# Sampled rows' weight stream: two tiles at each visit of TensorE, through the same three slots

## The chip, the cores and the metric

The kernel runs on one core of one Trainium2 chip. The metric is the device time of one execution in microseconds, compared by the medians of several runs. Profiles are taken on the same program.

## What is computed

One layer step for two kinds of rows, with shared weights: 1024 prompt rows and 8 sampled rows (one new token for each of 8 sequences with 4096 cached positions). The reference, cut down:

```python
q, k, v, logf, u = project(x, w_in, b_f)        # 1024 -> 3*512 + 8 + 512
attn = fox_prompt(q, k, v, logf)                # or fox_sample over the paged cache
pool = pool_mix(u_ext, start_pos, w_pool, pool_scale)
mix = concat(attn, pool) @ w_o                  # 1024 x 1024
x1 = layer_norm(ALPHA * x + mix, ln1_g, ln1_b)
hid = silu(x1 @ w_gate) * (x1 @ w_up)           # 1024 -> 2816
ffn = hid @ w_down                              # 2816 -> 1024
return layer_norm(ALPHA * x1 + ffn, ln2_g, ln2_b)
```

All data are float32. The prompt rows' products are made of three fp32r products each (high and low parts of both operands); the sampled rows' products use plain float32.

## The kernel before, in words

**The order of the work.** After attention the kernel runs one long sequence that is counted in *units* u. A unit is six fp32r matmuls of 512 columns for the feed-forward of the prompt rows. The 22 tiles of the hidden width give segments G (gate, 8 units each), U (up, 8 units) and D (down, 16 units for a pair of tiles); `segments()` writes their order out. Each engine walks through the same u in a loop of its own (`for u in range(LAST)`, on TensorE `for seg in SEGS`), and what else is to be done stands at a chosen u in front of or behind the unit's own work. Nothing is scheduled at run time: an engine that has to wait at one u holds up all that stands behind it in its own queue.

**The sampled rows.** Their 8 rows are multiplied with `w_o`, `w_gate`, `w_up` and `w_down` inside this sequence, from u = 386 on. The weights come as a stream of 37 tiles of 1 MB (`STREAM`, L169): four tiles W of `w_o`, then for each group g of four hidden tiles four GU tiles (two for the last, g = 5), and D tiles of `w_down` for the group before. `SUNIT` (L171) and `sample_steps()` (L147) say at which u each tile is used; before the change W tiles stand at u = 386, 388, 390, 392, and the 33 others from u = 406 to 504, about three units apart.

- `sample_tile(step)` (L1483) on TensorE waits until the tile has landed and runs four float32 products of 512 columns (eight of 256 for the last two GU tiles). They stand in four groups of 32 columns of the array and write to PSUM bank 6 (W and D, L1511) or bank 7 (GU, L1498). The profile shows each product as two matmuls, so a tile is 8 matmuls of 512 columns (or 16 of 256). One place of u where tiles are used is called a *visit* here; the last matmul of each tile increments `t_used`.
- Two units after the last GU tile of a group (`SUMS`), `sample_sum(g)` (L1516) on TensorE adds the partial products up. In front of it ScalarE has to copy them out of PSUM (`sample_partials`, L1094 with its copy at L1101, at SUMS - 1); ScalarE does at the same u what is due there before: `tile_hi` (L1013, its cast at L1026) makes the high part of the prompt rows' next weights, and waits for TensorE to end the segment whose weights it replaces. At SUMS + 1 ScalarE and VectorE make the hidden values, on which the next group's first GU tile and the group's own D tiles wait.
- SyncE issues the loads. `stream_tile(n)` (L643, its DMA at L652) has `TS = 3` slots; from the fourth tile on it waits until tile n - 3 has been used, and stands at one unit after that tile's visit. `weight_tile(e)` (L592, L596) loads the prompt rows' weights, 0.5 MB each, and waits until GpSimd has made the low part (`rest`, L807) of the tile three before; at an equal u it stands in front of the stream's load.

**Around the visits.** At u = 395 to 404 VectorE makes the first layer norm of the sampled rows (L2018 to L2036), TensorE turns them at u = 404 (L1533), and the second norm follows u = 506. The two norms stay at their u in the change.

Of the kernel before, what the change touches and what calls it, by code (L numbers as in the profile page):

```python
# [146 lines left out]
def sample_steps():  # L147


    order = []  # L150
    for g in range(TGROUPS):
        order += [("GU", g, r) for r in range(parts("GU", g))]
        order += [("D", g - 1, r) for r in range(parts("D", g - 1))] if g >= 1 else []
    order += [("D", TGROUPS - 1, r) for r in range(parts("D", TGROUPS - 1))]
    units = {step: TSTART + SPAN_S * n // (len(order) - 1) + 3 * (n >= parts("GU", 0)) for n, step in enumerate(order)}
    return units, [units["GU", g, parts("GU", g) - 1] + 2 for g in range(TGROUPS)]


def parts(kind, g):
    full = 4 * g + 4 <= FT  # L160
    return {"GU": (2, 4), "D": (1, 2)}[kind][full]
# [3 lines left out]
MIX, RESID, SQRT1, SCALE1, FACTORS1, OFFSETS1 = (CSPAD + n for n in (2, 11, 12, 13, 14, 18))  # L165
TURN1, TURNED1, TSTART = (CSPAD + n for n in (20, 21, 22))
SPAN_S = BEGIN["D", NPAIR - 1] - 11 - TSTART
STEPS_S, SUMS = sample_steps()
STREAM = [("W", n, 0) for n in range(4)] + list(STEPS_S)  # L169
TINDEX = {step: n for n, step in enumerate(STREAM)}  # L170
SUNIT = {("W", n, 0): MIX + 2 * n for n in range(4)} | STEPS_S  # L171
NORM2 = BEGIN["D", NPAIR - 1] + 2
SAMPLE2 = max(SUNIT.values()) + 2
LNVEC2 = BEGIN["U", FT - 1] + 2
# [36 lines left out]
def build(nc, t):  # L211
    ctx = ExitStack()
    with ctx:
# [259 lines left out]
        def _(sp):  # L473
# [169 lines left out]
            def stream_tile(n):  # L643
                if n < 2:
                    sp.wait_ge(k_red, NB * NKP)
                    if n == 1:
                        sp.wait_ge(m_sub, 2 * NB)
                elif n < TS:
                    sp.wait_ge(v_used, NB * NCH - 1)
                else:  # L650
                    sp.wait_ge(t_used, n - TS + 1)
                sp.dma_start(TR[n % TS], t["ws"][n]).then_inc(t_ld[n % TS], 16)  # L652

            for u in range(LAST):
# [18 lines left out]
                for n in range(TS, len(STREAM)):  # L673
                    if SUNIT[STREAM[n - TS]] + 1 == u:
                        stream_tile(n)
# [470 lines left out]
        def _(pe):  # L1146
# [369 lines left out]
            def sample_sum(g):  # L1516

                pe.wait_ge(e_gs, g + 1)
                for i in range(min(4, FT - 4 * g)):
                    ins = pe.matmul(PSM[:, 7, 2 * NB * i:2 * NB * (i + 1)], gu_s[:, i * P:(i + 1) * P], gumask[:],  # L1520
                                    start=True, stop=True)
                ins.then_inc(e_sum, 1)

            def sample(u):
                if u in SUMS:
                    sample_sum(SUMS.index(u))
                for step, at in SUNIT.items():
                    if at == u:
# [667 lines left out]
```

## Time and profile before

| what | value |
|---|---|
| time, three runs | 1450.91 us median (1446.38 to 1454.49) |
| the profiled execution's own time | 1451.53 us |
| its span, first to last instruction | 1449.0 us |
| granted TensorE clock, mean | 0.979 of full speed |
| TensorE matmuls busy | 1374.7 us (95% of the span) |
| VectorE, GpSimd, ScalarE busy | 48%, 37%, 25% |
| moved by DMA | 255.81 MB, 177 GB/s |

The profiled execution lies 0.62 us above the median of the runs; 2.5 us of its time lie outside the span. Rows of TensorE are named PE (matmuls) and PEld (weight loads). A matmul's shown duration overlaps the next one's, since its end is modelled; distances between starts are what tells its cost. Several neighbours of one kind stand in one row of the timeline as x2, x4 and so on.

### The profile page before, as it was taken

The numbers are of one execution on the slowest core, as the hardware profiler recorded it, in microseconds if no ns is written. First come the engines' busy times: TensorE is split into PE (matmuls) and PEld (weight loads), VectorE is DVE, ScalarE is ACT, GpSimd is POOL, SyncE is SP. The second block draws the span as 40 slices with busy tenths as digits, with TensorE's granted clock in tenths as the row PEclk, the third lists the DMA queues.
The fourth block names the chain that finished last, engine by engine and source line by source line (L and its number), as shares of the span: only waits on it lengthen the run. The fifth ranks groups of instructions, "written<-read, shape, count | busy, mean of one in ns | idle before, by whom it ended". The sixth has DMA issues, their size and how long they took to land.

```text
span 1449.0 us, 21271 instructions
## 1 busy us (share of the span) xinstructions
PE 1374.7 (95%) x7605; PEld 1081.9 (75%) x7605; DVE 695.4 (48%) x1043; ACT 359.9 (25%) x527; POOL 533.7 (37%) x250
## 2 busy tenths in 40 slices
PE   7899979989989899999999999999999999999996
PEld 5888879989869886676767676776767666666665
DVE  4746765874355683353536262544523142221336
ACT  4524334343331223111021211121120111111016
POOL 1016464742210035545565556555530212111114
PEclk9999999999989999999999999999999999999998
DMA  7244482731036115867676867768574644566522
GB/s 261 91 150 136 136 253 83 234 115 51 1 108 230 59 67 170 271 198 259 208 253 198 265 209 226 257 203 267 192 237 145 201 140 142 191 225 217 209 88 117
DMA packets 111913, 255.81 MB, mean 177 GB/s; under 512 B 12864, under 2 KB 23233, under 8 KB 106424
## 3 DMA queue, kind: packets, MB, share of 16 engines
q1 hardware_dynamic: 102528, 247.79, 51.4%
q10 hardware_dynamic: 8320, 4.19, 1.0%
q0 software_dynamic: 960, 2.47, 0.5%
q8 instruction: 60, 0.98, 0.3%
q14 instruction: 45, 0.37, 0.1%
HBM read 244.38 MB, written 10.25 MB: 176 GB/s over the span
## 4 chain that ended last, share of the span: by engine, by line
PE 77%; DVE 6%; SPq 5%; DMA 4%; issue 4%; POOL 3%; ACT 2%; ACTq 0%; DVEq 0%; POOLq 0%
PE PSM L1414 28%; PE PSM L1432 16%; PE PSM L1172 8%; PE PSM L1362 6%; PE PSM L1454 4%; PE PSM L1238 3%; PE PSM L1185 3%; SPq L477 2%; SPq L482 2%; PE PSM L1224 2%; PE PSM L1498 2%; POOL WR L755 1%; DMA AR<-cache_v 1%; PE PSM L1393 1%; PE PSM L1511 1%
## 5 line engine op out<-in xcount | busy, mean ns | idle before, releaser
L807 POOL TENSOR_TENSOR WL<-WR,WH 128x1024 fp32r<-128x1024 f32 x55 | 131.5, 2392 | 545.2 <-ACT WH L1026 545.2
L1414 PE MATMUL PSM<-XH,WH 128*128 128x512 f32 x672 | 221.2, 410 | 0.0
L755 POOL TENSOR_TENSOR AR<-AR,QB 128x1024 f32<-128x1024 f32 x80 | 196.2, 2471 | 43.9 <-DMA AR<-cache_k 32.0
L1414 PE MATMUL PSM<-XL,WH 128*128 128x512 f32 x672 | 212.0, 397 | 0.0
L1414 PE MATMUL PSM<-XH,WL 128*128 128x512 f32 x672 | 211.9, 397 | 0.0
L1414 PEld LDWEIGHTS PSM<-XH,WH 128*128 128x128 f32 x672 | 120.1, 189 | 88.0 <-issue 65.7
L1957 DVE TENSOR_TENSOR ACC<-ACC,PSM 128x512 f32<-128x512 f32 x160 | 108.3, 683 | 153.3 <-PE PSM L1432 152.9
L1414 PEld LDWEIGHTS PSM<-XH,WL 128*128 128x128 f32 x672 | 127.1, 189 | 30.4
L1432 PE MATMUL PSM<-R 128*128 128x512 f32 x528 | 149.7, 392 | 0.0
L1414 PEld LDWEIGHTS PSM<-XL,WH 128*128 128x128 f32 x672 | 127.2, 189 | 30.0
L1432 PE MATMUL PSM<-WH,R 128*128 128x512 f32 x352 | 143.2, 407 | 3.8 <-DVE R L1948 3.8
L1026 ACT CAST WH<-WR 128x1024 fp32r<-128x1024 f32 x55 | 57.5, 1047 | 327.8 <-PE PSM L1414 238.9
L1172 PE MATMUL PSM<-XH,WH 128*128 128x344 f32 x384 | 135.7, 353 | 0.0
L1944 DVE TENSOR_TENSOR AR<-AR,PSM 128x1024 f32<-128x1024 f32 x22 | 26.9, 1221 | 208.6 <-PE PSM L1414 201.6
L1172 PE MATMUL PSM<-XH,WL 128*128 128x344 f32 x384 | 125.0, 326 | 0.0
L1172 PE MATMUL PSM<-XL,WH 128*128 128x344 f32 x384 | 124.9, 325 | 0.0
L1432 PEld LDWEIGHTS PSM<-R 128*128 128x128 f32 x528 | 99.6, 189 | 22.1
L1594 DVE TENSOR_REDUCE AR<-AR 128x16 f32<-128x1024 f32 x64 | 77.6, 1212 | 64.6 <-POOL AR L755 64.1
L964 ACT ACTIVATE AR<-AR,negm 128x128 f32<-128x128 f32 (+3 forms) x64 | 49.8, 777 | 184.4 <-DVE negm L1685 184.4
L1432 PEld LDWEIGHTS PSM<-WH,R 128*128 128x128 f32 x352 | 66.5, 189 | 36.3 <-DVE ACC L1957 11.3
L755 POOL TENSOR_TENSOR ACC<-ACC,QB 128x1024 f32<-128x1024 f32 x24 | 58.8, 2459 | 72.0 <-issue 25.2
L1454 PE MATMUL PSM<-AR,PR 128*8 128x512 f32 x512 | 74.0, 598 | 5.3 <-DMA AR<-cache_v 5.3
(257 smaller groups left out, 2231.1 us busy)
## 6 DMA issues: line engine op xcount, KB each, us to landing
AR<-cache_v SPq DMA_DIRECT2D x256, 256.0 KB, 3.5
AR<-cache_k SPq DMA_DIRECT2D x160, 256.0 KB, 3.4
AR<-ws SPq DMA_DIRECT2D x37, 1024.0 KB, 4.9
WR<-ffn SPq DMA_DIRECT2D x66, 512.0 KB, 5.3
ACC<-cache_k SPq DMA_DIRECT2D x48, 256.0 KB, 3.0
WR<-cache_k SPq DMA_DIRECT2D x48, 256.0 KB, 3.0
WR<-w_in SPq DMA_DIRECT2D x20, 512.0 KB, 4.6
WR<-w_o SPq DMA_DIRECT2D x5, 1024.0 KB, 5.0
```

Of the source, the lines that this page charges most:

```text
L755: pool.tensor_tensor(keys, keys, QB[:].rearrange("p (o n) -> p o n", o=1).to_broadcast([P, KP, AW]), ALU.mult).then_inc(k_mul, 1)
L807: pool.tensor_tensor(lo, WR[:, raw_weight(e), :], hi.bitcast(F32), ALU.subtract).then_inc(ffn_lo, 1)
L964: act.activation(L[x % 2][:, 0:w], L[x % 2][:, 0:w], ACT.Exp, scale=-1.0, bias=negm[:, x % 2:x % 2 + 1], accum_out=rsum[:, x % 2:x % 2 + 1 ...
L1026: act.copy(weight_slot(kind, f)[0], WR[:, raw_weight(e), :]).then_inc(ffn_hi, 1)
L1172: ins = pe.matmul(third(n, m), w[a][:, tile_slot(n), k * P:(k + 1) * P], x[b][:, k, m * TH:(m + 1) * TH], start=(k == 0 and (a, b) == PART ...
L1185: ins = pe.transpose(TB[:, i * P:(i + 1) * P], src(i), ident[:])
L1362: ins = pe.matmul(output_bank(n), (XH, XL)[a][:, k, i * P:(i + 1) * P], wo[b][k // 4][:, k % 4, :], start=(r == 0 and at == 0), stop=(r == ...
L1414: ins = pe.matmul(out[:, hc], (hi, lo)[a][:, k * P:(k + 1) * P], x[b][:, k, hc], start=(k == 0 and n == 0), stop=(k == KC - 1 and n == 2))
L1432: ins = pe.matmul(PSM[:, 2 + n % 4, :], R2[:, 2 * r + a, i * P:(i + 1) * P], w[b][:, half * HALF:(half + 1) * HALF], start=(r == 0 and m = ...
L1454: ins = pe.matmul(PSM[32 * j:32 * j + H, 6, :], PR[:, c * CH + j, :], VR[c % 2][:, j * AW:(j + 1) * AW], start=(c == 0), stop=last, skip_g ...
L1594: dve.tensor_reduce(out[:, c * KP:(c + 1) * KP, :].rearrange("p j h -> p (j h)"), keys.rearrange("p (a n) -> p a n", n=HD), AX.X, ALU.add) ...
L1957: dve.tensor_tensor(cols, cols, PSM[:, 2 + n % 4, :], ALU.add).then_inc(d_free, 1)
```

## The change

Both formulas that place the tiles are changed, so that tiles 2m and 2m + 1 of the stream stand at one u, in front of the same unit. The four W tiles now stand at 386, 386, 390, 390. The 33 others stand in 16 pairs and a single tile, the pairs five or six units apart, from 406, 411, 420, 426, 432, 438 to 498, and the last tile at 504 as before. That gives 19 visits for 37 tiles. What is derived from it follows: the loads of two tiles stand together behind each visit; the sums' places (`SUMS`) become 413, 428, 446, 464, 482, 494 where they were 416, 431, 449, 467, 485, 497. The number of slots, the tiles, the matmuls and all waits are the same.

```diff
@@ sample_steps()
-    units = {step: TSTART + SPAN_S * n // (len(order) - 1) + 3 * (n >= parts("GU", 0)) for n, step in enumerate(order)}
+    units = {step: TSTART + SPAN_S * (n // 2) // (len(order) // 2) + 3 * (n >= parts("GU", 0)) for n, step in enumerate(order)}
     return units, [units["GU", g, parts("GU", g) - 1] + 2 for g in range(TGROUPS)]
@@
-SUNIT = {("W", n, 0): MIX + 2 * n for n in range(4)} | STEPS_S
+SUNIT = {("W", n, 0): MIX + 4 * (n // 2) for n in range(4)} | STEPS_S
```

## Rows read from the trace of the kernel before

**Rows 1.** Page: the chain that ended last, shares of the span by line

```profile
PE PSM L1414 28%; PE PSM L1432 16%; PE PSM L1172 8%; PE PSM L1362 6%; PE PSM L1454 4%; PE PSM L1238 3%; PE PSM L1185 3%; SPq L477 2%; SPq L482 2%; PE PSM L1224 2%; PE PSM L1498 2%; POOL WR L755 1%; DMA AR<-cache_v 1%; PE PSM L1393 1%; PE PSM L1511 1%
```

**Rows 2.** Busy times by stretch: us, busy us of each engine, granted clock, DMA share, GB/s

```profile
1216.00:1410.00 194.00, 191.72 (x960) 127.27 (x960) 43.51 (x58) 26.59 (x35) 29.55 (x12) 1.00 0.55 193
```

**Rows 3.** Chain that ended last, in order of time: start, us, what

```profile
1315.37 4.40 PE PSM L1414 x18
...
1343.10 4.31 PE PSM L1432 x18
```

**Rows 4.** Timeline of PE, units of U and G: start, us, what

```profile
1191.82 0.63 PE L1414 MATMUL PSM<-XH,WH 128*128 128x512 f32 x2
...
1205.75 0.63 PE L1414 MATMUL PSM<-XH,WH 128*128 128x512 f32 x2
...
1241.49 1.06 PE L1498 MATMUL PSM<-AR,GB 128*32 128x512 f32 x8
...
1246.88 1.06 PE L1498 MATMUL PSM<-AR,GB 128*32 128x512 f32 x8
```

**Rows 5.** Timeline of PE in parts: the two packs of a 512-column tile

```profile
1231.06 0.64 PE L1498 MATMUL PSM<-AR,GB 128*32 128x512 f32 x4
...
1231.51 0.61 PE L1498 MATMUL PSM<-AR,GB 128*32 128x512 f32 x4
```

**Rows 6.** Timeline of PE in parts: third and fourth pack of a 256-column tile

```profile
1375.33 0.40 PE L1498 MATMUL PSM<-AR,GB 128*32 128x256 f32 x4
...
1375.54 0.40 PE L1498 MATMUL PSM<-AR,GB 128*32 128x256 f32 x4
```

**Rows 7.** Timeline of PE, the sums of groups 2 and 5

```profile
1293.85 0.62 PE L1414 MATMUL PSM<-XH,WL 128*128 128x512 f32 x2
1295.71 1.06 PE L1520 MATMUL PSM<-gumask_sb,QB 128*128 128x16 f32 x8 [1.24 <-ACT QB L1101]
...
1383.68 0.61 PE L1414 MATMUL PSM<-XH,WL 128*128 128x512 f32 x2
1385.34 0.62 PE L1520 MATMUL PSM<-gumask_sb,QB 128*128 128x16 f32 x4 [1.05 <-ACT QB L1101]
```

**Rows 8.** Timeline of ACT at the same two places

```profile
1294.14 1.03 ACT L1026 CAST R<-WR 128x1024 fp32r<-128x1024 f32 x1
1295.08 0.57 ACT L1101 COPY QB<-PSM 128x512 f32<-128x512 f32 x1
...
1384.92 0.36 ACT L1101 COPY QB<-PSM 128x256 f32<-128x256 f32 x1
```

**Rows 9.** The loads into the stream's slots, from issue to landing, all 37

```profile
DMA to landing us min/median/max: 4.7/4.9/7.3
```

**Rows 10.** Loads by line: KB, us to landing; issued at 1282.03, then at 1299.41

```profile
WR<-ffn SPq DMA_DIRECT2D x1, 512.0 KB, 5.7
...
AR<-ws SPq DMA_DIRECT2D x1, 1024.0 KB, 6.8
```

**Rows 11.** Timeline of SP behind the visit at u = 450

```profile
1296.69 2.67 SPq L596 DMA_DIRECT2D WR<-ffn  x2
1299.41 0.43 SPq L652 DMA_DIRECT2D AR<-ws  x1
```

**Rows 12.** Timelines of DVE and PE around the turn at u = 404

```profile
1196.44 1.21 DVE L2033 TENSOR_TENSOR AR<-AR 8x1024 f32<-8x1024 f32 x1
1201.86 1.22 DVE L1944 TENSOR_TENSOR AR<-AR,PSM 128x1024 f32<-128x1024 f32 x1 [4.21 <-PE PSM L1414]
...
1209.83 1.01 PE L1533 MATMUL PSM<-ident_sb,AR 8*128 8x8 f32 x8 [2.52 <-DVE AR L2036]
```

**Rows 13.** Busy times by stretch, behind that turn

```profile
1209.90:1216.10 6.20, 6.20 (x20) 4.65 (x20) 0.23 (x1) 0.00 (x0) 0.00 (x0) 0.50 0.22 82
```

**Rows 14.** Weight loads of the GU tiles: ns min/median/max, first and last start

```profile
L1498 PEld LDWEIGHTS PSM<-AR,GB x192: 106/109/154, 1216.2 to 1380.7; 128*32 128x32 f32 x192
```

## The prediction

> **What bounds the kernel now.** I read the page's chain first, then the busy times by stretch, the chain in order of time, and last the starts of single matmuls on PE, because only distances between starts tell what a visit costs.
>
> The chain that ended last runs mostly over PE [rows 1]. In the stretch that holds most of the stream, 1216 to 1410, PE is busy 191.7 of 194 us at the full granted clock, all others at most 23%, and the DMA engines 55% [rows 2]. There the chain is PE alone, the tiles' matmuls in turns with three units (18 matmuls) in 4.40 us for G and U or 4.31 us for D [rows 3]. So each us that PE is spared ends the kernel earlier, as long as no load and no other engine takes its place. The change adds and removes no matmul; what it can change is the cost of going into and out of the tiles, the places where PE waits, and whether tiles are there in time.
>
> **What a visit costs.** Ten units of G and U without a visit take 1205.75 - 1191.82 = 13.93 us, so a unit is 1.39 us [rows 4]. From one visit to the next with three units between them there are 1246.88 - 1241.49 = 5.39 us; less 3 x 1.39 a visit costs 1.21 us [rows 4]. I take 1.20, since a D stretch has slightly shorter units. 37 visits are 44 us.
>
> **What the second tile of a visit costs.** The matmuls of a tile go in packs of four that start together. The second pack of a 512-column tile starts 1231.51 - 1231.06 = 0.45 us behind the first [rows 5]. Two packs at that distance are 0.90 us, so 0.30 us of the visit are entry and exit. No visit of before has four packs of 512 columns, but the last GU tiles have four of 256: the last two are 1375.54 - 1375.33 = 0.21 us apart [rows 6]. For twice the columns that is 0.43 us (0.42 to 0.43 by rounding), 0.86 for the two packs. The second tile therefore adds 0.86 (by rows 6) to 0.90 us (by rows 5), and a merged visit saves 0.34 to 0.30 us. I take 0.34, since rows 6 show packs in the third and fourth place, with other weights than the two before them, which is exactly what a second tile is. The far ends: it may save nothing (the second tile also needs the landing of its load and pays its own entry), or, if half of the entry and exit were hidden as well, no more than 0.4. There are 18 merged visits: **18 x 0.34 = 6.1 us** (5.4 by rows 5; ends 0 and 7.2).
>
> The Trainium skill says (TensorEngine Tiling (Array Packing), Tiling Modes) that changing the tiling mode drains the array, while changing tiles within a mode does not. That gives the reason for an entry and an exit that one visit pays once, and no other number.
>
> **The sums.** Six times TensorE runs `sample_sum`, two units behind the last GU tile. At group 2 (u = 449) it starts at 1295.71, while the pair of matmuls before it started at 1293.85 and would let it start 0.46 us later: 1.4 us lost, released by ScalarE's copy. At group 5 (u = 497) the same gives 1385.34 - 1384.14 = 1.2 us [rows 7]. ScalarE was late there because the copy stands at u = 448 and 496, where two casts for new weights are due before it, and these wait for the end of a segment: the copy began at 1295.08 and 1384.92 right behind them [rows 8]. Groups 0, 1, 3 and 4 lose nothing. In the change the copies stand at u = 412, 427, 445, 463, 481, 493, the sums one unit later. The casts stay at 408, 416, 424, 440, 448, 456, 464, 472, 488, 496. None shares a u with a copy or stands directly in front of one; the nearest in front is three units (4.2 us) away, against at most two casts (2 us) and a silu. So both waits go: **2.6 us**. Ends: 0, if a new place waits (it would be behind another cast), and 2.6. What is late next at these places is nothing that PE needs soon: the low half of the hidden tile, needed a segment later.
>
> **Loads.** Tile 2m + 3 goes into the slot of tile 2m, and its load is released when that first tile of the visit is used, not at the visit's end: 1.1 us behind the visit's start, the 1.06 us of its matmuls [rows 4] and some hundredths for the signal. It is used as second tile of the next visit. From visit to visit lie 6 x 1.39 + 2.06 = 10.4 us (2.06 = 1.20 + 0.86), plus 0.89 until the second tile begins, less 1.1: 10.2 us are left. With five units (406 to 411) it is 8.8, and for W (four D units of 1.37) 7.3. The loads took 4.7 to 7.3 us, median 4.9 [rows 9]. Tile 2m + 4 is issued 0.9 us behind and has a whole period more. Two such loads stand behind each other now. A 0.5 MB load that was issued 1.2 us behind a stream tile landed after 5.7 us [rows 10], so a second load queues behind the first, by an amount that the longer time covers. I cost the loads at 0; what hides them is 2.9 us of slack even at the longest load seen, and for W 2.4 us at the median. Weight loads of the prompt rows that queue behind 2 MB are some 3 us later; the next user is 12 units or more away.
>
> One place is tight: at u = 451 SP first waits for GpSimd and issues two weight loads, at 1296.69 and 2.3 us later, and only then the stream's tile at 1299.41 [rows 11], which landed 6.8 us later [rows 10]. Unit 448 ended at 1294.31, where the sum could have started, and so began at 1292.92; the landing at 1306.2 is 13.3 us behind that. In the change the second tile at u = 456 begins 2 x 1.39 + 0.1 + 10.4 + 0.9 = 14.2 us behind it. 0.9 us of slack: at 0, end 1 us lost.
>
> **The turn at u = 404.** PE waits 2.52 us there for VectorE, and that wait [rows 12] stays: the norm's chain was through with L2033 at 1197.65 and VectorE then idle 4.21 us until PE ended U16. In the change the last W tile ends two units earlier but the chain still starts behind the last D unit: about 0.8 us later against PE, covered by these 4.2 us. Behind the wait the granted clock was 0.50, the 1.2 GHz level, for 6.2 us [rows 13]; that stretch can be a few us longer or shorter from run to run, and I put nothing on it. The tail (one tile at 504, norm at 506) is not moved.
>
> **Sum.** 6.1 + 2.6 = 8.7 us against the profiled execution's 1451.53: 1442.8 us. The median of the runs stands 0.6 lower, at 1450.91; I say 1442.2, 0.60% less. A measurement of this kernel can tell about 0.5% (7.3 us) from no change, so the forecast stands only 1.4 us beyond that line, and the three runs of before spread over 8.1 us.
>
> **Rivals.**
> 1. *The second tile's weight loads are not hidden.* Each pack loads 32 columns four at a time, 109 ns each [rows 14]. If two packs paid that in each merged visit, 0.22 of the 0.34 us would go: 18 x 0.12 + 2.6 = 4.8 us, 1446.1. Against it: third and fourth pack of rows 6 are 0.21 us apart although their weights are loaded meanwhile. Chance 0.08.
>  The Trainium skill has such a rule (TensorE: Matmul & The Clock Gate, Part 3, What overlaps and what doesn't): weight loads overlap running matmuls only if their row group differs, and all these tiles use all rows. By that rule this rival holds; the distances of rows 6 don't bear it out.
> 2. *The visit pays entry and exit per tile*, because the second tile's wait for its load breaks the stream: only the sums gain, 1448.3. Against it: each D unit also has waits that were long fulfilled, and its three units take 4.31 us without a gap [rows 3]. Chance 0.06.
> 3. *The sums wait at a new place*, or their gain is lost to another wait: 6.1 us alone, 1444.8. Chance 0.06.
> 4. *Slower: the tile in the second half of a visit lands late.* This is one mechanism: a load that shares the DMA engines with another 1 MB beside it. It decides from 10.2 us after issue on. If it landed after 12 us, 17 visits would lose 1.8 us each, 31 us, for 1442.2 + 31 = 1473; to be over 0.5% slower it takes 16 us in all, a landing after 11.1 us. Against it: longest load 7.3 us [rows 9], DMA engines 55% busy [rows 2], and more bytes in the same time are not moved. Chance 0.04.
>
> **Numbers.** Forecast 0.76. With the runs' spread it falls beyond 0.5% in about 7 of 10: 0.54, plus a little of rival 3, gives faster 0.56. Same: the rest of the forecast and rivals 1 to 3, 0.40. Slower 0.04. The range: down to 1438.0, which is 1450.9 less the far ends 7.2 + 2.6 and 3 us of the runs' spread; up to 1448.5, which takes in rivals 1 to 3.
>
> **What would show it.** Right: 19 groups x16 (two x32) of L1498 and L1511 but the last, about 2.06 us from entry to exit; packs 0.43 us apart; no wait of L1520 for ACT; landings below 10 us; the wait of 2.5 us in front of L1533 unchanged. Wrong: PE idle with DMA as the releaser in front of L1498 or L1511, a low granted clock between 1216 and 1410, or packs of a second tile 0.5 us and more behind the first's.

## The result, and the profile after

| | before | changed |
|---|---|---|
| median of 8 runs each | 1446.82 us (1442.58 to 1454.49) | 1436.22 us (1433.34 to 1441.16) |
| ratio, 95% interval | | 0.9922 (0.9895 to 0.9949) |
| two more comparisons (12 and 11 runs of the changed kernel) | | 0.9950 (0.9924 to 0.9976), 0.9938 (0.9914 to 0.9962) |
| profiled execution, span | 1451.53, 1449.0 us | 1433.34, 1431.5 us |

The change makes the kernel faster: all three intervals lie below 1. One more run of the last comparison, a slow one of 5730.55 us, is left out. The three comparisons have a mean ratio of 0.9937, that is 9.1 us of 1447; the forecast was 8.7 us, 0.60%. The forecast time and the range were nevertheless missed: 1436.22 lies below 1438.0. Why is told below; the larger part of it was not one of the terms of the sum.

The page of the changed kernel, its chain by line (it answers to [rows 1]):

```profile
span 1431.5 us, 21271 instructions
...
PE PSM L1414 30%; PE PSM L1432 16%; PE PSM L1172 8%; PE PSM L1362 6%; PE PSM L1454 4%; PE PSM L1238 3%; PE PSM L1185 3%; PE PSM L1224 2%; SPq L477 1%; PE PSM L1498 1%; SPq L482 1%; PE PSM L1393 1%; POOL WR L755 1%; PE PSM L1511 1%; DMA AR<-cache_v 1%
```

The share of the chain that goes over the stream's tiles fell (L1498 from 2% to 1%), and no other share moved by more than two points.

**The visits.** The chain in order of time shows two visits of the changed kernel, and the timeline of PE, cut into parts, the packs inside another one (start, us, what; only the starts are read, since the x at the end counts what the part held):

```profile
1295.49 1.85 PE PSM L1498 x16
1297.34 8.57 PE PSM L1414 x36
1305.91 1.85 PE PSM L1498 x16
```

```profile
1231.42 0.64 PE L1498 MATMUL PSM<-AR,GB 128*32 128x512 f32 x4
...
1232.30 1.03 PE L1498 MATMUL PSM<-AR,GB 128*32 128x512 f32 x6
...
1232.73 0.61 PE L1498 MATMUL PSM<-AR,GB 128*32 128x512 f32 x4
1233.27 0.73 PE L1414 MATMUL PSM<-XH,WH 128*128 128x512 f32 x2
```

The second tile begins 1232.30 - 1231.42 = 0.88 us behind the first, and its second pack 0.43 us later. From visit to visit with six units between lie 1305.91 - 1295.49 = 10.42 us; less 6 x 1.39 a double visit costs 2.08 us by these rounded rows (2.06 with the unit at 1.393). That is the forecast price.

**The sums.** In the list of who waited for whom, from the tiles' start on, TensorE's own waits for another engine are now only these (us in total, times, longest), and L1520 is not among them:

```profile
PE PSM L1432 <- DVE R L1948: 3.8, 1, 3.8
PEld PSM L1533 <- DVE AR L2036: 2.9, 1, 2.9
PE PSM L1533 <- DVE AR L2036: 2.5, 1, 2.5
```

Both waits of [rows 7] are gone, and the wait at the turn is the 2.5 us of [rows 12].

**The loads.** Issue to landing of all 37 loads into the slots:

```profile
DMA to landing us min/median/max: 4.7/6.4/8.4
```

Then the two that stand behind the weight loads at u = 451: the timeline of SP, the landing of each (KB, us), and the second tile's weight loads at u = 456 (timeline of PEld):

```profile
1289.64 0.91 SPq L652 DMA_DIRECT2D AR<-ws  x2
...
AR<-ws SPq DMA_DIRECT2D x1, 1024.0 KB, 5.7
...
AR<-ws SPq DMA_DIRECT2D x1, 1024.0 KB, 7.8
...
1296.30 0.13 PEld L1498 LDWEIGHTS PSM<-AR,GB 128*32 128x32 f32 x4 [0.30 <-issue]
```

The median rose from 4.9 to 6.4 us [rows 9], since the second load of a pair queues behind the first: behind the visit at u = 406 they landed 4.9 and 7.7 us after their issue. None is waited for. The first of the two loads at u = 451 is the second tile of u = 456; it landed at 1289.64 + 5.7 = 1295.3, 1.0 us before its use at 1296.30, where the forecast left 0.9. The other is the first tile of u = 462 and has a period more.

**The granted clock.** The busy times by stretch, columns as in [rows 2], behind the turn at u = 404:

```profile
1203.40:1209.60 6.20, 6.20 (x40) 3.80 (x41) 0.22 (x1) 0.00 (x0) 0.00 (x0) 1.00 0.40 103
```

Where the kernel before ran at 0.50 [rows 13], this execution ran at the full clock, behind the same wait. This, and an earlier start of the stream (1171.69 against 1177.49, with no changed instruction ahead of it), is what the two profiles' spans differ by beyond the forecast.

### The profile page after: what moved, and what is told of

It is laid out like the page before. It is cut to its first block, busy times and chain, and to the rows that moved or that the text cites. A ratio compares the mean times of both kernels' runs of the same rounds, so it can differ in the third digit from the quotient of the medians.

```text
span 1431.5 us, 21271 instructions
## 1 busy us (share of the span) xinstructions
PE 1359.9 (95%) x7605; PEld 1077.4 (75%) x7605; DVE 696.9 (49%) x1043; ACT 360.2 (25%) x527; POOL 534.1 (37%) x250
## 4 chain that ended last, share of the span: by engine, by line
PE 78%; DVE 8%; DMA 4%; SPq 3%; issue 3%; POOL 2%; ACT 2%; ACTq 0%; DVEq 0%; POOLq 0%
PE PSM L1414 30%; PE PSM L1432 16%; PE PSM L1172 8%; PE PSM L1362 6%; PE PSM L1454 4%; PE PSM L1238 3%; PE PSM L1185 3%; PE PSM L1224 2%; SPq L477 1%; PE PSM L1498 1%; SPq L482 1%; PE PSM L1393 1%; POOL WR L755 1%; PE PSM L1511 1%; DMA AR<-cache_v 1%
## 5 line engine op out<-in xcount | busy, mean ns | idle before, releaser
L1432 PE MATMUL PSM<-R 128*128 128x512 f32 x528 | 149.7, 392 | 0.0
L1432 PE MATMUL PSM<-WH,R 128*128 128x512 f32 x352 | 142.9, 406 | 4.8 <-DVE R L1948 3.8
L1432 PEld LDWEIGHTS PSM<-R 128*128 128x128 f32 x528 | 99.7, 189 | 22.4
L1944 DVE TENSOR_TENSOR AR<-AR,PSM 128x1024 f32<-128x1024 f32 x22 | 26.9, 1221 | 164.0 <-PE PSM L1414 157.0
L1432 PEld LDWEIGHTS PSM<-WH,R 128*128 128x128 f32 x352 | 66.5, 189 | 34.0 <-issue 17.8
```

The costliest lines, as they stand in the source:

```text
L1432: ins = pe.matmul(PSM[:, 2 + n % 4, :], R2[:, 2 * r + a, i * P:(i + 1) * P], w[b][:, half * HALF:(half + 1) * HALF], start=(r == 0 and m = ...
```

## Experiments

All profiles are compared over one stretch: from the start of the first tile to the start of the last row of L1432 on PE. It is 1437.12 - 1177.49 = 259.63 us for the kernel before and 1419.71 - 1171.69 = 248.02 us for the changed one:

```profile
1171.69 0.64 PE L1511 MATMUL PSM<-AR,GB 128*32 128x512 f32 x4
...
1419.71 0.84 PE L1432 MATMUL PSM<-R 128*128 128x512 f32 x3
```

"Low" below is the time in this stretch at the 1.2 GHz level, without the one behind the last wait, the 3.8 us of L1432 for VectorE. That one is 3.4 us long in every profile but e5's, where it is 6.8.

**e1: the pairs, with the sums where they were.**

```diff
-    return units, [units["GU", g, parts("GU", g) - 1] + 2 for g in range(TGROUPS)]
+    before = {step: TSTART + SPAN_S * n // (len(order) - 1) + 3 * (n >= parts("GU", 0)) for n, step in enumerate(order)}
+    return units, [before["GU", g, parts("GU", g) - 1] + 2 for g in range(TGROUPS)]
```

> The pairs of the change, but the sums, their copies and their silus at the units of before (416, 431, 449, 467, 485, 497). If the two parts of the sum are independent (visits 6.1 us, sums 2.6 us), this kernel keeps the visits' part alone: 19 visits of which 18 cost 2.06 us, the waits of L1520 for ScalarE's copy at groups 2 and 5 are back with 1.4 and 1.2 us, and the time is 2.6 us above the changed kernel's and some 6 us (0.4%) below the kernel before. Rival: the sums' waits came from the tile's late end and not from the casts in front of the copy; then they stay away here too, since the last GU tile now ends three units earlier, and the time equals the changed kernel's.

Measured: ratio 0.9958 (0.9928 to 0.9989), 1442.87 us, median of 12 runs. The waits for the copy are back at groups 2 and 5, 2.3 us on PE (and 3.1 us on PEld, in the same time) as in the kernel before, though the tile now ended three units earlier:

```profile
1295.03 1.06 PE L1521 MATMUL PSM<-gumask_sb,QB 128*128 128x16 f32 x8 [1.24 <-ACT QB L1102]
```

So they come from ScalarE's casts in front of the copy and not from the tile; the rival falls. And one thing that the prediction had not priced: the clock fell behind this wait, and the next visit, of 16 matmuls, took 2.94 us in place of 1.92 (busy times by stretch, then timeline of PE):

```profile
1211.40:1218.20 6.80, 6.79 (x24) 4.93 (x28) 0.22 (x1) 0.00 (x0) 0.00 (x0) 0.50 0.22 79
1296.80:1300.20 3.40, 3.40 (x16) 1.14 (x18) 2.70 (x2) 0.00 (x0) 1.52 (x1) 0.50 0.67 213
```

```profile
1298.09 2.94 PE L1512 MATMUL PSM<-AR,SC 128*32 128x512 f32 x16
```

**e2: the kernel before, with ScalarE's copy in front of the casts.** Only the order within one u is changed:

```diff
             for u in range(LAST):
                 b, o = divmod(u, WIN)
+                for g in range(TGROUPS):
+                    if SUMS[g] - 1 == u:
+                        sample_partials(g)
                 if u > 0 and u in TURN_U:
                     rows_hi(TURN_U[u])
...
                 for g in range(TGROUPS):
-                    if SUMS[g] - 1 == u:
-                        sample_partials(g)
                     if SUMS[g] + 1 == u:
                         sample_silu(g)
```

> The kernel before, with the single tiles, but at each unit ScalarE makes the copy for the sum before the casts that are due at the same unit. If the casts in front of the copy were what TensorE waited for, the waits of L1520 at groups 2 and 5 go (1.4 and 1.2 us) and the kernel is 2.6 us (0.2%) faster than before, with 37 visits of 1.20 us unchanged. Rival: the casts are only moved behind the copy and hold up something that TensorE needs soon (high part of the weights, hidden tile); then a new wait of about 0.5 us each stands elsewhere and the gain is nearer 1.5 us.

Measured: ratio 0.9998 (0.9970 to 1.0026). By time alone this tells nothing, since the expected 0.9982 and no change are both inside. By the profile the waits are gone; the sum of group 2 follows the last matmul pair at once, and the casts behind the copy hold up nothing: TensorE's list of waits has only those of the turn and of the last D segment (timeline of PE, then of ACT):

```profile
1288.94 0.63 PE L1415 MATMUL PSM<-XH,WL 128*128 128x512 f32 x2
1289.40 0.96 PE L1521 MATMUL PSM<-gumask_sb,QB 128*128 128x16 f32 x8
```

```profile
1286.66 0.59 ACT L1101 COPY QB<-PSM 128x512 f32<-128x512 f32 x1 [12.02 <-PE PSM L1499]
1288.27 1.06 ACT L1026 CAST WH<-WR 128x1024 fp32r<-128x1024 f32 x1 [1.02 <-PE PSM L1415]
```

**e3, e8, e10: the changed kernel again; e6, e7: the kernel before again.** No edit.

> The changed kernel once more, for a second profile. The profiled execution of the changed kernel had no stretch of low granted clock behind the turn at u = 404, the one of the kernel before had 6.8 us of it. If that is chance (where the wait falls in time), this profile may show 0, 3.4 or 6.8 us of it, and over the runs the change is worth about 8.7 us. Rival: the change removes it always, then every profile of the changed kernel is free of it and the change is worth about 11.5 us. Visits 2.06 us, no wait of L1520 for the copy in either case.

> A second profile of the kernel before, for the granted clock behind the turn at u = 404. If a low stretch there is chance, it may have 0, 3.4 or 6.8 us; if the kernel before always has it, 3.4 us or more again. From the first tile of the stream to the last product of TensorE: 257.2 us plus about 0.43 of each us at the low clock.

> A third profile of the kernel before, with the same expectations as for the second.

> A third profile of the changed kernel. Two profiles had no low clock behind the turn. If that is chance, this one may show 3.4 or 6.8 us; if the change removes it, none. The stretch from the first tile of the stream to the last product of TensorE: 248.5 us, and about 0.43 of each us at the low clock more.

> The changed kernel again, on one chip with e9, for the size of the change. If the parts found in the profiles are all of it (visits 6.1, sums 2.6 us, and a low clock behind the sum of group 2 in some executions of the kernel before, about 1 us in the mean), it is 9 to 10 us below the kernel before, a ratio of 0.993 to 0.994. Rival: the first measurement's 0.9922 was the true size; then 11 us and more.

Measured: e3 0.9950 (0.9924 to 0.9976), e10 0.9938 (0.9914 to 0.9962); e6, e7 and e8 are one execution each. Together with the others:

| profile | stretch, us | low behind the turn | low behind the sum of group 2 | stretch less 0.44 x low |
|---|---|---|---|---|
| before | 259.63 | 6.8 | 0 | 256.6 |
| e6, before | 258.35 | 0 | 3.4 | 256.9 |
| e7, before | 259.88 | 3.4 | 3.4 | 256.9 |
| changed | 248.02 | 0 | 0 | 248.0 |
| e3, changed | 248.04 | 0 | 0 | 248.0 |
| e10, changed | 248.03 | 0 | 0 | 248.0 |
| e8, changed | 251.04 | 6.8 | 0 | 248.0 |
| e1, pairs alone | 255.36 | 6.8 | 3.4 | 250.9 |
| e2, sums alone | 255.37 | 3.4 | 0 | 253.9 |

The price of a low us comes from e8 against the changed kernel: (251.04 - 248.02) / 6.8 = 0.44. The row of e8 behind its turn, and that of e7 behind its sum:

```profile
1206.20:1213.00 6.80, 6.80 (x24) 4.85 (x28) 0.23 (x1) 0.00 (x0) 0.00 (x0) 0.50 0.20 75
```

```profile
1293.90:1297.30 3.40, 3.40 (x13) 1.15 (x11) 3.01 (x2) 0.00 (x0) 1.83 (x1) 0.50 0.64 187
```

With that taken out, the three profiles of before agree within 0.3 us. The three of the changed kernel without a low stretch agree within 0.02 us; e8 gave the price and so checks nothing. The difference is 256.8 - 248.0 = 8.8 us, where the forecast has 8.7; e1 gives 5.9 us for the visits (forecast 6.1), e2 2.9 us for the sums (forecast 2.6), each from one profile. The low clock behind the turn comes and goes from one execution to the next in both kernels (2 of 3 profiles of before, 1 of 4 of the changed one), so it is not removed by the change; whether it comes less often is not shown by so few. Behind the sum of group 2 it fell in three of four profiles with that wait (before, e6, e7, e1), and in none of the others. Three quarters of 3.4 x 0.44 us is 1.1 us: a rough estimate, from four profiles, of what the change gains besides. 8.8 + 1.1 = 9.9 us are 0.9932, inside all three intervals. The rival of e10, 11 us and more, is not borne out, though its interval alone does not shut it out.

**e4: VectorE's last addition of the first sampled norm three units earlier.**

```diff
-MIX, RESID, SQRT1, SCALE1, FACTORS1, OFFSETS1 = (CSPAD + n for n in (2, 11, 12, 13, 14, 18))
+MIX, RESID, SQRT1, SCALE1, FACTORS1, OFFSETS1 = (CSPAD + n for n in (2, 11, 12, 13, 14, 15))
```

> The changed kernel with VectorE's last addition of the first sampled norm (L2036) at u = 399 in place of 404, in front of the prompt rows' product at u = 400. VectorE was idle for 3.4 us there. If the wait of 2.5 us in front of L1533 comes from that addition standing behind the hidden tile's low half in VectorE's queue, it goes: about 2.9 us less than the changed kernel, and also no low granted clock behind the turn in any profile. Rival: the addition waits for ln1_b to land and holds up the product at u = 400, so that half or more of the gain is lost.

Measured: ratio 0.9897 (0.9852 to 0.9941), 1431.12 us; stretch 245.43, 2.6 us less than the changed kernel's. By the constants (384 + 18, then 384 + 15) the addition moved from u = 402 to 399; the 404 of the expectation is the unit of the turn. It waited 2.0 us for `ln1_b`, as the rival has it, but in time that was idle, and held up nothing. The addition now fills VectorE's idle time and L1944 follows it (timeline of DVE):

```profile
1193.80 1.21 DVE L2036 TENSOR_TENSOR AR<-AR 8x1024 f32<-8x1024 f32 x1 [2.02 <-DMA AR<-ln_b]
1195.19 1.22 DVE L1944 TENSOR_TENSOR AR<-AR,PSM 128x1024 f32<-128x1024 f32 x1 [0.18 <-PE PSM L1414]
```

It took 1.21 us here, 3.38 where it stood before (why was not tried). No wait stands in front of L1533, and no low clock behind it.

**e5: the changed kernel with two slots for the stream.**

```diff
-TS = 3
+TS = 2
...
                 if u == (NB - 1) * WIN + VLOAD[-1]:
-                    stream_tile(2)
                     sp.wait_ge(v_used, NB * NCH)
```

> The changed kernel with two slots for the stream in place of three: both tiles of a visit are loaded behind the visit before. The first is issued 1.1 us and the second 2.0 us behind that visit's start; in the changed kernel such pairs landed 4.8 to 6.5 and 6.4 to 8.4 us after issue. Needed are they after 10.4 and 11.3 us (five units: 9.0 and 9.9; W: 7.5 and 8.4). So if loads have the slack that the prediction says, waits for loads come to at most 3 us in all, nearly all of them at W, at u = 411 and at u = 456, and the time is 0 to 3 us above the changed kernel's. Rival (a late second tile makes it slow): more than 1 us of wait at each of 17 visits, and 15 us or more above the changed kernel's.

Measured: ratio 0.9958 (0.9929 to 0.9987), 1442.38 us; stretch 250.83, 2.8 us above the changed kernel's. Waits for loads came up, few and short (who waited for loads of the stream; us, times, longest):

```profile
PEld PSM L1497 <- DMA AR<-ws: 3.7, 3, 2.5
PE PSM L1497 <- DMA AR<-ws: 1.6, 1, 1.6
PEld PSM L1510 <- DMA AR<-ws: 0.7, 1, 0.7
```

The four waits stand where the expectation puts them: at the second W visit, at u = 411 and at both tiles of u = 456. Only the last place costs PE anything. There the visit begins 0.2 us late and its second tile 2.66 us behind the first, in place of 0.88 (timeline of PE):

```profile
1304.70 1.07 PE L1497 MATMUL PSM<-AR,GB 128*32 128x512 f32 x8
...
1307.36 1.06 PE L1497 MATMUL PSM<-AR,GB 128*32 128x512 f32 x8 [1.59 <-DMA AR<-ws]
```

That is 2.0 of the 2.8 us; the other 0.8 is the longer low clock behind the last wait, which this profile alone has. So with a slot less the stream costs 2 us at one place, not the 15 of the rival. With three slots that place has 1.0 us left and all others more.

**e9: e4, and the last addition of the second sampled norm one unit earlier.**

```diff
-                if u == SAMPLE2 + 6:
+                if u == SAMPLE2 + 5:
                     dve.wait_ge(e_g1, 2)
```

> The kernel with VectorE's addition at u = 399 (as in e4) and also the last addition of the second sampled norm one unit earlier, at u = 511, in front of the prompt rows' last product at u = 512 instead of behind it. There it stood for 1.2 us in the chain to the last D segment. If VectorE's place in the queue is what counts, the wait in front of the last D segment falls from 3.8 to 2.6 us and the kernel is 1.2 us below e4, some 16 us (1.1%) below the kernel before. Rival: ln2_b has not landed at u = 511 and the product at 512 is held up; then nothing is gained or up to 1 us is lost against e4.

Measured: ratio 0.9887 (0.9855 to 0.9918), 1432.85 us; stretch 245.25, only 0.2 us below e4. The wait in front of the last D segment stayed at 3.8 us. My expectation was wrong: the addition had stood beside ScalarE's cast, for which L1948 waits anyway (timelines of DVE and ACT of e9):

```profile
1403.71 1.22 DVE L1944 TENSOR_TENSOR AR<-AR,PSM 128x1024 f32<-128x1024 f32 x1 [1.03 <-PE PSM L1414]
1406.04 1.22 DVE L1948 TENSOR_TENSOR R<-AR,R 128x1024 fp32r<-128x1024 f32 x1 [1.11 <-ACT R L1062]
```

```profile
1404.96 1.04 ACT L1062 CAST R<-AR 128x1024 fp32r<-128x1024 f32 x1 [7.91 <-DVE AR L1944]
```

So e9 and e4 are the same within what can be told, and both beat the kernel before. The medians of e4 and e9 are 7.7 and 8.5 us below those of the changed kernel in the same comparisons (1438.79 and 1441.38), of which the stretch shows 2.6 and 2.8. The rest goes with a higher mean granted clock of their six runs each (0.984 and 0.983, against 0.981 and 0.980); that the edit causes it is not shown.

## Why the prediction was right in its sum and wrong in its number

- **What bounds the kernel: right.** What PE was spared came off the end, us for us, at the full clock.
- **The second tile at 0.86 us, a double visit at 2.06: right.** The rows show 0.88 us to the second tile and 0.43 us between its packs; e1 has 5.9 us for 18 merged visits. Reading the price from four packs of 256 columns, and not from the two of 512, was the better choice. Rivals 1 and 2 fall, and by the lists of waits 3 and 4 too. By the rule on row groups (the Trainium skill, TensorE: Matmul & The Clock Gate, Part 3) a second tile would have added an estimated 0.22 us more (two loads of 109 ns, [rows 14]); the measured distance leaves no room for it. The rule on mode changes (the Trainium skill, TensorEngine Tiling (Array Packing), Tiling Modes) agrees with an entry and exit of some 0.3 us paid once a visit.
- **The sums, 2.6 us: right, and cut too short.** Cause and size stand (e1, e2: 2.9 us). I had 2.6 as the upper end. The clock falls behind the wait of group 2 in most profiles that have it, about 1.1 us more in the mean; I had looked at the clock behind the turn alone, because the one profile of before happened not to show it elsewhere.
- **Loads at 0: right.** The longest took 8.4 us (9.3 in e8) where 10.2 were left, and nobody waited. The tight place at u = 456 was read rightly: 1.0 us left, forecast 0.9. With a slot less (e5) it is the one place that costs time.
- **The turn: right.** The wait stayed at 2.5 us. That its low clock varies was said; e6 and e8 show it in both kernels.
- **From the sum to the time and the range: this failed.** The forecast was put on the median of three runs, 1450.91. With five more runs it was 1446.82, and in later comparisons, on three chips, 1447.79, 1447.59 and 1450.62 (29, 13 and 17 runs). On 1446.82 the sum gives 1438.1. I had seen that the three runs spread over 8.1 us and yet took only 3 us of spread into the range, and none for the base itself. That is 4 of the 6 us missed. About 1 us more is a term that I had put at nothing: the low clock behind the sum of group 2. The last 1 us is within the measurement's own interval, 0.27% or 4 us either way, and stays open. In the second and third comparison the changed kernel took 1438.79 and 1441.38 us, within the range; in the third, with the base at 1450.62, it is 0.8 us from the forecast, which is luck of the base as much as the first miss was. That the time would fall by more than 0.5% was the likelier case, with 0.56, and it came so in the first comparison (0.78%) and the third (0.62%), on the edge in the second (0.50%).

## What to carry to other kernels

A detour of an engine costs its work and a fixed entry and exit; read the work's price from the steadiest part of the longest detour there is, and what merging saves is the difference. Where an engine waits at a sum or a turn, look what stands in front of the releasing instruction in its own queue: moving the copy by units, or in front of the casts, was worth half of what the merging was (2.9 and 5.9 us). And a forecast of a time needs a range for its base: when the effect is as large as the spread of three runs, say the difference and put the base's spread into the range.

## What the runs showed that was not expected

Most of the spread of this kernel goes with the granted clock. The 12 runs of e1, one program on one chip, go from 1432.58 us at a mean granted clock of 0.988 to 1449.34 at 0.978. At 0.44 us for each us at the low level the 0.010 between them is some 13 of these 16.8 us, an estimate. In the profiles the first tile of the stream starts between 1171.14 (e6) and 1184.76 us (e9), though all instructions ahead of it are the same: 13.6 us, more than the whole change. Ahead of it e6 has 34.1 us at the low clock and e9 51.2, which at the same price is 7.5 of the 13.6; what the rest is was not traced. A comparison of two profiles' spans (17.5 us here) is therefore no measure of a change of 9; the same stretch, with the low clock taken out, agrees within 0.3 us.

The wait of PE at the turn, 2.5 us by the profile, was followed by 0, 3.4 or 6.8 us at 1.2 GHz; the one at the sum of group 2, 1.2 us, by 0 or 3.4 us; and the one at the sum of group 5, 1.0 us, by none in the four profiles that have it. So a wait of 1.2 us, too, is enough in some executions. What decides it was not tried.
